# Joint mix of a two-stream transformer kernel: pair-wise attention steps, and 16 modulation units moved to the wide up stage

## The chip, the core and the metric

The kernel runs on one NeuronCore of a Trainium2 chip. TensorE (PE) multiplies matrices into eight PSUM banks of 512 fp32 columns; VectorE (DVE), ScalarE (ACT) and GpSimd (POOL) work on SBUF, the first two on PSUM too; SyncE (SP) issues the DMAs. Each engine runs its own queue in order and waits for the others by semaphores. The metric is the device time of one launch in microseconds (us), as the median of several runs.

## The reference

A transformer on 256 tokens of 1024 features, all in fp32. `first_block` has two layers. `second_block` has two more over two streams, 256 latent and 256 context tokens, each with modulation from a conditioning vector:

```python
mod_l = jnp.split(silu(c) @ ada_w[l] + ada_b[l], 6)          # the same for c_ctx: six parts of 1024
hl = modulate(x_lat, norm_g[l, 0], mod_l[0], mod_l[1])       # rms norm, scale, shift; hc likewise
mix_c, mix_l = even_mixer(hc, hl, ...)                       # layer 0; odd_mixer in layer 1
x_lat = x_lat + mod_l[2] * (mix_l @ w_out[l])
x_lat = x_lat + mod_l[5] * conv_ffn(modulate(x_lat, norm_g[l, 1], mod_l[3], mod_l[4]), ...)
```

`even_mixer` has two halves. One is a bidirectional mLSTM of four heads of width 128, in chunks of 128 tokens: per chunk the query-key products times a decay matrix, the state carried on, and a stabilised division. The other is attention of eight heads of width 64 with a learnt sink in the softmax: the context tokens attend to themselves, the latent tokens to the context and to a window of their own. Its output, the mLSTM's normed output beside it, goes through `w_out`. `conv_ffn` is an up projection to 2 x 2816 features, a depthwise convolution of width 3 on both halves, silu(gate) x value, and a down projection.

## The kernel before, in words

**Products with weights.** All weights stream through a ring of `SLOTS` = 3 slots of 1 MB, issued by SP in the order of the list `issue` (L2902); the DMA into a slot waits until PE has read the slot's former content. Each weight matrix comes in halves. ACT makes the high part of a half (`ahead`, L357; `HIGHS` = 4 halves in flight), GpSimd the low part (`lows_G`, L364), and PE makes three matmuls of each product (`product`, L370 to L372). `done(...)` names the semaphore count of a step that is noted, so that the program's order in each queue is the order in which the Python code writes it.

**Stages.** The layers of the second block are called 2.0 and 2.1. For layer 2.0 the stages are "2.0 in" (projection to the mixers' inputs, six cuts of four pieces for the tiles of 128 tokens, each read out of its bank by DVE, L748, or ACT, L751), "2.0 attention" (the joint mix), "2.0 out", "2.0 ffn up" (22 column blocks f of 2 x 128 features over all 512 tokens) and "2.0 ffn down".

**The joint mix** weaves three generators in each engine's queue (`both_of`): attention, recurrence and modulation, one slot each at a time, 23 slots of recurrence, five per head. In four of five slots there is an attention step too; what is left of attention runs after the recurrence.
- Attention (`att_T`, `att_V`, `att_A`): 32 jobs, one head and one query tile each, first the context stream's 16 (256 keys), then the latent stream's 16 (512 columns, masked). At step s PE makes the scores of job s (L918), the turn (transpose) of job s-3 (L927) and the values' sum of s-4 (L942); DVE takes the minimum of job s (L964, masked L960; signs are turned) and scales the probabilities of s-2 (L975 to L981); ACT makes exp (L1006), the sink's exp (L1009) and copies the turned rows (L1017). Rows have four buffers (`NB`). From job 21 on, scores take three banks in turn and turns two.
- Recurrence (`mlstm_T`, `mlstm_V`, `mlstm_A`): chunk sums (L2060), query-key products (L2069), ACT's decay rows (L2100, L2103), DVE's product with them (L2150) and the finishing steps (L2117 to L2134). Its output goes on over GpSimd (`mout_G`) and DVE (`mout_sum_V`, at given steps of attention, `MOUT_AT`).
- Modulation (`late_mod_T`, `late_mod_V`): `LATE_MOD` lists ten (layer, part) pairs of four units, 40 units of 1 MB. Each is streamed through the ring and multiplied with silu(c) (L1663, 16 matmuls), two or three half units a slot in the loop, by `LATE_TURNS`. A finished part is added to its bias by DVE (`mod_rows_V`, L1683), and parts 0, 1, 3 and 4 are also laid flat by PE and DVE (`mod_flat_T`, `mod_flat_V`). The sums alternate between banks 0 and 6.

**The wide up stage.** `up_T` makes block f into banks 2(f mod 4) and 2(f mod 4)+1, after the hidden low of block f-4 (L1525). `up_A` makes, for each block in this order: the high of half 2f+4 of the stage (in the slot of block f+2), the mids of both halves (L1514), the high of half 2f+5, silu (L1518) and the hidden high (L1520). `up_V_both` makes four convolution steps (L1561, L1564), then the hidden low of block f-1 (L1525), then the product (L1572):

```python
            for f in range(FC):
                ahead(A, m0 + 2 * f + 1 + HIGHS)
                A.eng.wait_ge(tensor_done, done("T", ph, "up", f))
```

**An earlier stage with units behind its blocks.** "1.0 ffn up" (256 tokens) already multiplies eight modulation units behind column blocks; they are streamed into two slots of their own in `work` by DMAs of L2885. Layer 2.1's mixer already uses steps of pairs of heads (`pair_T` L1206, `pair_V`, `pair_A`, `tile_pairs`): its turns are L1221, its scores L1251, its sums L1276.

## Time and profile before

| | |
|---|---|
| time, median of 3 runs | 1874.07 us (1873.81 to 1883.03) |
| the profiled execution: its time | 1877.97 us |
| its span | 1876.1 us |
| mean granted PE clock | 0.98 of full speed |
| first scores of the mix to "2.0 out" | 863.7 to 1043.0 us |
| busy: PE, ACT, DVE, GpSimd | 94%, 48%, 40%, 51% of the span |

A row of the timeline has the start in us from the span's start, the duration, the engine, the line of the kernel, the operation and its tiles; in brackets the time that the engine had stood idle before, and the step that ended it. A matmul row with xN is N matmuls of the same kind in line.

### The profile page before, as it was taken

How to read it: one execution, taken by the hardware profiler on the slowest of the kernel's cores; microseconds unless marked ns; L12 is line 12 of the kernel's file. 1: busy time of each engine (PE TensorE's matmuls, PEld its weight loads, DVE VectorE, ACT ScalarE, POOL GpSimd, SP SyncE). 2: the span in 40 equal slices, each digit the busy share in tenths (PEclk: the TensorE clock that was granted, in tenths of full speed). 3: DMA queues.
4: the chain of work that ended last, by engine and by line, in shares of the span. 5: the costliest groups of instructions: out<-in, count | busy, mean ns of one | idle time of the engine just before them, and what ended most of it. 6: DMA issues, size and time to landing. Idle time of an engine off the chain costs nothing.

```text
span 1876.1 us, 25748 instructions
## 1 busy us (share of the span) xinstructions
PE 1767.1 (94%) x10058; PEld 1438.4 (77%) x10058; DVE 751.9 (40%) x1655; ACT 905.7 (48%) x1654; POOL 947.6 (51%) x416
## 2 busy tenths in 40 slices
PE   8999999998899999898998999999999898899998
PEld 6668998776688888785555888888888877678886
DVE  4543231244344453743567143343200443346631
ACT  4655454445566743433335354444422454457762
POOL 4645688774278885331015234444343341238886
PEclk9999999999899999999999999999999999999999
DMA  8336765443156653227875133333232430136654
GB/s 271 102 102 215 244 186 176 168 157 113 56 163 186 182 177 105 77 90 247 286 275 180 51 85 90 90 109 94 90 101 79 108 106 24 45 92 192 188 169 146
DMA packets 264843, 263.48 MB, mean 140 GB/s; under 512 B 11332, under 2 KB 202124, under 8 KB 264596
## 3 DMA queue, kind: packets, MB, share of 16 engines
q1 hardware_dynamic: 264435, 261.25, 45.0%
q8 instruction: 80, 1.31, 0.3%
q10 hardware_dynamic: 288, 0.59, 0.1%
q14 instruction: 40, 0.32, 0.1%
HBM read 260.76 MB, written 1.06 MB: 140 GB/s over the span
## 4 chain that ended last, share of the span: by engine, by line
PE 80%; DVE 7%; ACT 5%; DMA 5%; issue 2%; SPq 1%; POOL 0%; ACTq 0%; DVEq 0%
PE bank L370 18%; PE bank L371 18%; PE bank L372 17%; PE bank L1447 8%; PE bank L1448 4%; PE bank L1663 2%; PE bank L1251 2%; DMA weights<-in_ada_w 2%; ACT work L1369 1%; PE bank L1221 1%; ACT weights_high L357 1%; PE bank L2060 1%; PE bank L918 1%; PE bank L942 1%; DVE work L1330 1%
## 5 line engine op out<-in xcount | busy, mean ns | idle before, releaser
L364 POOL TENSOR_TENSOR weights_low<-weights,weights_high 128x1024 fp32r<-128x1024 f32 (+1 forms) x388 | 918.7, 2382 | 767.4 <-ACT weights_high L357 766.9
L357 ACT ACTIVATE weights_high<-weights 128x1024 fp32r<-128x1024 f32 (+1 forms) x388 | 401.6, 1046 | 377.8 <-PE bank L372 122.1
L370 PE MATMUL bank<-weights_high,normed_features_high_low 128*128 128x512 f32 (+4 forms) x752 | 288.9, 384 | 14.6 <-POOL weights_low L364 5.6
L372 PE MATMUL bank<-weights_low,normed_features_high_low 128*128 128x512 f32 (+4 forms) x752 | 273.8, 364 | 0.0
L371 PE MATMUL bank<-weights_high,normed_features_high_low 128*128 128x512 f32 (+4 forms) x752 | 273.7, 364 | 0.0
L1447 PE MATMUL bank<-normed_features_high_low,weights_high 128*128 128x512 f32 x704 | 249.4, 399 | 0.6 <-DVE normed_features_high_low L499 0.4
L370 PE MATMUL bank<-normed_features_high_low,weights_high 128*128 128x256 f32 (+1 forms) x704 | 237.9, 338 | 0.4 <-DVE normed_features_high_low L497 0.2
L371 PE MATMUL bank<-normed_features_high_low,weights_low 128*128 128x256 f32 (+1 forms) x704 | 236.5, 336 | 0.0
L372 PE MATMUL bank<-normed_features_high_low,weights_high 128*128 128x256 f32 (+1 forms) x704 | 236.5, 336 | 0.0
L1448 PE MATMUL bank<-normed_features_high_low,weights_low 128*128 128x256 f32 x704 | 197.7, 281 | 0.0
L370 PEld LDWEIGHTS bank<-weights_high,normed_features_high_low 128*128 128x128 f32 x752 | 144.9, 193 | 46.4 <-issue 13.6
L370 PE MATMUL bank<-weights_high,hidden_high 128*128 128x512 f32 x440 | 172.9, 393 | 2.8 <-DVE hidden_low_narrow L1525 1.0
L372 PE MATMUL bank<-weights_low,hidden_high 128*128 128x512 f32 x440 | 171.3, 389 | 0.0
L372 PEld LDWEIGHTS bank<-weights_low,normed_features_high_low 128*128 128x128 f32 x752 | 144.4, 192 | 21.3
L1447 PEld LDWEIGHTS bank<-normed_features_high_low,weights_high 128*128 128x128 f32 x704 | 132.3, 188 | 34.3 <-DVE normed_features_high_low L499 0.5
L371 PEld LDWEIGHTS bank<-weights_high,normed_features_high_low 128*128 128x128 f32 x752 | 145.1, 193 | 17.0
L370 PEld LDWEIGHTS bank<-normed_features_high_low,weights_high 128*128 128x128 f32 x704 | 133.6, 190 | 17.7 <-issue 3.3
L372 PEld LDWEIGHTS bank<-normed_features_high_low,weights_high 128*128 128x128 f32 x704 | 133.6, 190 | 13.6
L371 PEld LDWEIGHTS bank<-normed_features_high_low,weights_low 128*128 128x128 f32 x704 | 133.6, 190 | 13.5
L1448 PEld LDWEIGHTS bank<-normed_features_high_low,weights_low 128*128 128x128 f32 x704 | 133.0, 189 | 0.0
L371 PE MATMUL bank<-weights_high,hidden_low_narrow 128*128 128x512 f32 x264 | 102.8, 389 | 0.0
L370 PEld LDWEIGHTS bank<-weights_high,hidden_high 128*128 128x128 f32 x440 | 82.6, 188 | 23.3 <-POOL weights_low L364 2.2
(330 smaller groups left out, 2334.1 us busy)
## 6 DMA issues: line engine op xcount, KB each, us to landing
weights<-in_ffn_w_up SPq DMA_DIRECT2D x44, 1024.0 KB, 6.1
weights<-in_ffn_up SPq DMA_DIRECT2D x44, 1024.0 KB, 6.0
weights<-in_ada_w SPq DMA_DIRECT2D x40, 1024.0 KB, 6.3
weights<-in_ffn_w_down SPq DMA_DIRECT2D x20, 1024.0 KB, 5.1
weights<-in_ffn_down SPq DMA_DIRECT2D x20, 1024.0 KB, 5.0
weights<-in_diff_w_qkv SPq DMA_DIRECT2D x12, 1024.0 KB, 5.2
weights<-in_hyb_w_in SPq DMA_DIRECT2D x11, 1024.0 KB, 5.5
weights<-in_odd_w_in SPq DMA_DIRECT2D x9, 1024.0 KB, 5.2
```

Source lines behind the costliest of these rows:

```text
L357: A.eng.activation(high(whigh[:, m % HIGHS, :]), raw(wslot[:, u % SLOTS, :]), ACT.Copy).then_inc(scalar_done, A.one(("A", "high", m)))
L364: G.eng.tensor_tensor(raw(wlow[:, u % SLOTS, :]), raw(wslot[:, u % SLOTS, :]), high(whigh[:, m % HIGHS, :]).bitcast(F32), ALU.subtract).th ...
L370: T.eng.matmul(out_, lh, rh, start=first, stop=False)
L371: T.eng.matmul(out_, ll, rh, start=False, stop=False)
L372: return T.eng.matmul(out_, lh, rl, start=False, stop=last)
L918: i = T.eng.matmul(bank[:, a:b], l, r, start=(m == 0), stop=(m == len(terms) - 1))
L942: i = T.eng.matmul(o, l, r, start=(first and c == 0), stop=(last and c == nc_ - 1))
L1221: i = T.eng.transpose(psum[TURNED][:, at:at + P], way["probs"](buffer(way, q, x), n)[:, c * P:(c + 1) * P], ident)
L1251: i = T.eng.matmul(psum[SCORES[x]][:, a:b], l, r, start=(m == 0), stop=(m == len(terms) - 1))
L1447: T.eng.matmul(bank[:, 0:2 * n].rearrange("p (h t) -> p h t", h=2), wh, nTb[:, :, k, lo:lo + n], start=first, stop=False)
L1448: return T.eng.matmul(bank[:, 0:n], wl, nTh[:, k, lo:lo + n], start=False, stop=last)
L1663: i = T.eng.matmul(to[32 * j:32 * j + 32, :], silu_k[:, k, 2 - 2 * layer:34 - 2 * layer], w[:, a, j * MOD_N:(j + 1) * MOD_N], start=(k == ...
```

## The change

1. **Attention of the joint mix by pairs.** The 32 jobs become 16 steps, each of the two heads of one tile (`tile_pairs`). A step has two half-steps, each taking one slot of `both_of`. In the first PE makes the scores of pair s into banks 3 and 4. In the second it turns pair s-1 into bank 0, for 256 columns both heads at once and one wait, for 512 head by head, each after ACT has copied the one before. When s-2 was a group's second tile, it then sums the group over both tiles, 256 columns wide, into bank 7. DVE takes the maxima of s in the first half and scales the probabilities of s-1 in the second; ACT makes exp in the first and copies the turned rows of s-1 in the second. There are two buffers for each head's rows.
2. **Modulation.** `LATE_MOD` has 24 units, one in each of the first 24 calls, all in bank 6, so that a part waits until DVE has read the one before; the flats of four parts come together at the end in bank 5. The other 16, parts 2 to 5 of layer 2.1 (`UP_MOD`), stream through the ring between the weights of blocks 0 to 15 of "2.0 ffn up", one behind each block, and are multiplied behind it into banks 6 and 7. That stage has three blocks in flight in place of four. DVE adds a part's rows at f = 4, 8, 12 and 16.
3. **"2.0 in".** The pieces of cuts 2 and 3 are all read by ACT. ACT makes a weight high between the two directions of the gates' logarithms; the turns L852 of the second group start a slot later; the exp table is loaded ahead of the last copies; the mix's first modulation matmul waits for DVE's last piece only. The DMAs that bring decay rows in come at the first and the third unit.
4. The down stage's and gates' banks of 2.0 are permuted, since banks 6 and 7 are free earliest.

The core of the diff:

```diff
-        LATE_MOD = [(0, i) for i in range(2, 6)] + [(1, i) for i in (0, 1, 3, 2, 4, 5)]
+        LATE_MOD = [(0, i) for i in range(2, 6)] + [(1, i) for i in (0, 1)]
+        UP_MOD = [(1, i) for i in range(2, 6)]
...
+                if f < len(between) * MOD_UNITS:
+                    layer, idx = between[f // MOD_UNITS]
+                    up_unit[f] = len(stream)
+                    stream.append((mod_source(layer, idx, f % MOD_UNITS), mod_view))
+                    issue.append(("weights", len(stream) - 1))
...
-        add_up("2.0 ffn up", io["ffn_up_2"][0])
+        add_up("2.0 ffn up", io["ffn_up_2"][0], between=UP_MOD)
...
+        def att_T(T, ph, steps):
+            count, held = len(steps), None
+            for s in range(count + 3):
+                if s < count:
+                    j = steps[s]
+                    if s >= 1:
+                        e = "V" if steps[s - 1]["mask"] is not None else "A"
+                        T.eng.wait_ge(SEM[e], done(e, ph, "read", s - 1, 1))
+                    for (a, b, terms), (_, _, others) in zip(j["heads"][0]["scores"], j["heads"][1]["scores"]):
...
                 yield
+                if 0 <= s - 1 < count:
+                    q = s - 1
+                    n = steps[q]["n"]
+                    for heads in heads_of(n):
+                        if held is not None:
+                            T.eng.wait_ge(scalar_done, done(*held))
+                        for x in heads:
+                            T.eng.wait_ge(vector_done, done("V", ph, "probs", q, x))
+                            for c in range(n // P):
+                                at = (x * n if len(heads) == 2 else 0) + c * P
+                                i = T.eng.transpose(psum[TURNED][:, at:at + P], rows_of(q, x, n)[:, c * P:(c + 1) * P], ident)
...
+                        held = ("A", ph, "turned", q, heads[-1])
+                if 0 <= s - 2 < count and steps[s - 2]["tile"] == 1:
...
+        def in_flight(ph):
+
+            return 3 if ph == "2.0 ffn up" else 4
...
+                if ph == "2.0 ffn up" and f in up_unit:
+                    up_mod_T(T, f)
+                if ph == "2.0 ffn up" and f - 6 in up_flats:
+                    mod_flat_T(T, *up_flats[f - 6], up_sums(f - 6)[1])
...
+        def up_mod_T(T, f):
+
+
+            (layer, idx), unit, u = UP_MOD[f // MOD_UNITS], f % MOD_UNITS, up_unit[f]
+            T.eng.wait_ge(slot_full[u % SLOTS], 16 * (u // SLOTS + 1))
+            if unit == 0 and f >= 2 * MOD_UNITS:
+                before = UP_MOD[f // MOD_UNITS - 2]
+                T.eng.wait_ge(vector_done, done("V", "mod flat" if before[1] in FLAT else "mod rows", *before))
+            for a in range(2):
+                i = mod_unit_T(T, layer, unit, mod_view(wslot[:, u % SLOTS, :]), a, up_sums(f)[0])
+            i.then_inc(tensor_done, T.one(("T", "slot", u)))
...
+        LATE_TURNS = [2] * 24
...
             for d in range(2):
                 log_sigmoid(None, A, ph, d, None, mrow(d, 2), mrow(d, 3))
+                if d == 0:
+                    ahead(A, first_half["2.0 in"] + 14)
...
-        proj_phase("2.0 in", ("2.0 norm", ALL, shift_scale(0, 0)), EVEN_CUTS, lambda c: ALL, even_dst, lambda c, j: "A" if c == 4 else "VA"[j % 2],
+        proj_phase("2.0 in", ("2.0 norm", ALL, shift_scale(0, 0)), EVEN_CUTS, lambda c: ALL, even_dst, lambda c, j: "A" if c in (2, 3, 4) else "VA"[j % 2],
...
-            both_of(att_V(V, ATTN, js + jl, aside), mlstm_V(V, ML), late_mod_V(V))
+            both_of(att_V(V, ATTN, js + jl, aside), mlstm_V(V, ML), late_mod_V(V), True)
```

## Rows read from the trace of the kernel before

**Rows 1.** The page's head and busy times of the engines.

```profile
span 1876.1 us, 25748 instructions
...
PE 1767.1 (94%) x10058; PEld 1438.4 (77%) x10058; DVE 751.9 (40%) x1655; ACT 905.7 (48%) x1654; POOL 947.6 (51%) x416
```

**Rows 2.** Sums by stretch: us, busy by engine, granted clock, DMA share, GB/s.

```profile
864.00:979.00 115.00, 99.83 (x852) 57.62 (x854) 59.96 (x203) 44.44 (x146) 7.52 (x6) 0.96 0.82 292
979.00:1043.00 64.00, 56.12 (x393) 35.12 (x385) 43.91 (x93) 29.50 (x66) 28.12 (x20) 0.92 0.48 158
1110.00:1360.00 250.00, 250.00 (x1104) 206.96 (x1103) 94.46 (x132) 108.31 (x141) 107.81 (x45) 1.00 0.34 97
919.00:942.50 23.50, 21.81 (x197) 12.86 (x197) 15.42 (x49) 9.24 (x32) 2.50 (x2) 1.00 0.84 298
```

**Rows 3.** Timeline of PE: a gap in "2.0 in", and the first modulation matmul.

```profile
786.67 0.80 PE L370 MATMUL bank<-weights_high,normed_features_high_low 128*128 128x512 f32 x1 [5.43 <-DVE big L748]
...
866.74 0.65 PE L1663 MATMUL bank<-weights,silu_wide 128*32 128x256 f32 x4 [2.36 <-ACT big L751]
```

**Rows 4.** Timeline of PE: first scores, a late job's scores, first product of "2.0 out".

```profile
863.69 0.70 PE L918 MATMUL bank<-qk_features 64*128 64x256 f32 x2
...
979.80 1.12 PE L918 MATMUL bank<-qk_features 64*128 64x512 f32 x2
...
1042.97 0.58 PE L370 MATMUL bank<-weights_high,normed_features_high_low 128*128 128x512 f32 x1
```

**Rows 5.** Timeline of PE in the loop: a modulation unit and chunk sums.

```profile
944.90 1.07 PE L1663 MATMUL bank<-weights,silu_wide 128*32 128x256 f32 x16
...
947.48 2.50 PE L2060 MATMUL bank<-big,work 128*128 128x129 f32 x20
```

**Rows 6.** Timeline of PE in the mix of layer 2.1: turns and sums of pairs.

```profile
1558.57 0.60 PE L1221 MATMUL bank<-con,work 128*128 128x128 f32 x4
...
1567.49 1.95 PE L1276 MATMUL bank<-work,big 128*64 128x256 f32 x16
```

**Rows 7.** Timeline of DVE and ACT in the loop: softmax steps and a decay product.

```profile
906.34 0.42 DVE L964 TENSOR_REDUCE mxs<-bank 128x1 f32<-128x256 f32 x1
...
906.87 0.15 DVE L975 TENSOR_TENSOR mxs<-mxs 128x1 f32<-128x1 f32 x1
...
906.98 0.48 ACT L1006 ACTIVATE attention_rows<-bank,mxs 128x256 f32<-128x256 f32 x1 [3.12 <-DVE mxs L967]
...
909.71 0.69 DVE L2150 TENSOR_TENSOR work<-bank,gate_rows 128x512 f32<-128x512 f32 x1 [0.36 <-ACT gate_rows L2103]
```

**Rows 8.** Timeline of DVE and GpSimd in the mix's tail.

```profile
1020.22 2.23 DVE L975 TENSOR_TENSOR mxs<-mxs 128x1 f32<-128x1 f32 x1
...
1020.08 2.35 POOL L364 TENSOR_TENSOR weights_low<-weights,weights_high 128x1024 fp32r<-128x1024 f32 x1 [1.46 <-ACT weights_high L357]
```

**Rows 9.** DMA issues at 1163.89, 171.00 and 205.6: KB, us to landing.

```profile
weights<-in_ffn_up SPq DMA_DIRECT2D x1, 1024.0 KB, 6.0
...
work<-in_ada_w SPq DMA_DIRECT2D x1, 1024.0 KB, 7.6
...
work<-in_ada_w SPq DMA_DIRECT2D x1, 1024.0 KB, 9.6
```

**Rows 10.** Timeline of SP in "1.0 ffn up": weights and a unit issued in line.

```profile
169.97 0.61 SPq L2902 DMA_DIRECT2D weights<-in_ffn_w_up  x1
171.00 1.51 SPq L2885 DMA_DIRECT2D work<-in_ada_w  x1
```

**Rows 11.** Timeline of ACT and DVE in "2.0 ffn up": one block, and the next block's mids.

```profile
1163.90 0.78 ACT L1514 ACTIVATE gate_rows<-bank,convcol 128x512 f32<-128x512 f32 x1 [3.76 <-PE bank L372]
...
1165.24 1.06 ACT L357 ACTIVATE weights_high<-weights 128x1024 fp32r<-128x1024 f32 x1
...
1167.80 0.68 DVE L1525 TENSOR_TENSOR hidden_low_wide<-bank,hidden_high 128x512 fp32r<-128x512 f32 x1
...
1174.78 1.45 ACT L1514 ACTIVATE gate_rows<-bank,convcol 128x512 f32<-128x512 f32 x2 [3.82 <-PE bank L372]
```

More of the change, by code:

```diff
@@ new lines, in att_V @@
+        def att_V(V, ph, steps, aside):
+            count = len(steps)
+            for s in range(count + 3):
+                if s < count:
+                    j = steps[s]
+                    V.eng.wait_ge(tensor_done, done("T", ph, "turn", s - 2, 1))
+                    for x, head in enumerate(j["heads"]):
+                        b = 2 * (s % 2) + x
+                        mn = mxs[:, b:b + 1]
+                        bank = psum[SCORED[x]][:, 0:j["n"]]
+                        V.eng.wait_ge(tensor_done, done("T", ph, "scores", s, x))
+                        if j["mask"] is not None:
+                            V.eng.tensor_tensor_reduce(out=rows_of(s, x, j["n"]), in0=bank, in1=j["mask"], scale=1.0, scalar=head["sink"],
+                                                       op0=ALU.add, op1=ALU.min, accum_out=mn).then_inc(vector_done, V.one(("V", ph, "read", s, x)))
+                        else:
+                            V.eng.tensor_reduce(mn, bank, AX_X, ALU.min).then_inc(vector_done, V.one())
+                            V.eng.wait_ge(vector_done, V.n)
+                            V.eng.tensor_tensor(mn, mn, head["sink"], ALU.min).then_inc(vector_done, V.one())
+                        V.note(("V", ph, "max", s, x))
@@ L985, in att_V @@
-                if s >= LOW and jobs[s - LOW]["close"] is not None:
-                    j = jobs[s - LOW]
-                    src_cols, high, low = j["close"]
-                    if low is not None:
-                        V.eng.wait_ge(scalar_done, done("A", ph, "group", j["group"]))
-                        V.eng.tensor_tensor(low, psum[SUM_BANK][:, src_cols], high.bitcast(F32), ALU.subtract).then_inc(vector_done, V.one(("V", ph, "group", j["group"])))
-                yield
-        def att_A(A, ph, jobs, aside={}):
-            n = len(jobs)
-            for s in range(n + LOW):
+                yield
@@ new lines, in att_V, with att_A @@
+                if 0 <= s - 3 < count and steps[s - 3]["close"] is not None:
+                    j = steps[s - 3]
+                    cols, high, low = j["close"]
+                    V.eng.wait_ge(scalar_done, done("A", ph, "group", j["group"]))
+                    V.eng.tensor_tensor(low, psum[SUMMED][:, cols], high.bitcast(F32), ALU.subtract).then_inc(vector_done, V.one(("V", ph, "group", j["group"])))
+                yield
+        def att_A(A, ph, steps, aside):
+            count = len(steps)
+            for s in range(count + 3):
+                if s < count:
+                    j = steps[s]
+                    if j["mask"] is None:
+                        A.eng.wait_ge(tensor_done, done("T", ph, "turn", s - 2, 1))
+                    for x, head in enumerate(j["heads"]):
+                        b = 2 * (s % 2) + x
+                        mn = mxs[:, b:b + 1]
+                        A.eng.wait_ge(vector_done, done("V", ph, "max", s, x))
+                        pb = rows_of(s, x, j["n"])
+                        A.eng.activation(pb, pb if j["mask"] is not None else psum[SCORED[x]][:, 0:j["n"]], ACT.Exp, bias=mn, scale=-1.0,
+                                         accum_out=mxs[:, 8 + b:9 + b]).then_inc(scalar_done, A.one(("A", ph, "read", s, x)))
+                        A.eng.activation(mxs[:, 16 + b:17 + b], head["sink"], ACT.Exp, bias=mn, scale=-1.0).then_inc(scalar_done, A.one(("A", ph, "exp", s, x)))
+                if 0 <= s - 3 < count and steps[s - 3]["close"] is not None:
+                    j = steps[s - 3]
+                    cols, dst, _ = j["close"]
+                    A.eng.wait_ge(tensor_done, done("T", ph, "sum", j["group"]))
+                    A.eng.activation(dst, psum[SUMMED][:, cols], ACT.Copy).then_inc(scalar_done, A.one(("A", ph, "group", j["group"])))
@@ L1279, in pair_T @@
                             l, r = (pt, head["v"][c]) if tok else (head["v"][c], pt)
-                            i = T.eng.matmul(psum[SUMMED][rows_, cols], l, r, start=(first and c == 0), stop=(last and c == n // P - 1))
+                            i = T.eng.matmul(psum[way["sum_bank"]][rows_, cols], l, r, start=(first and c == 0), stop=(last and c == n // P - 1))
                     i.then_inc(tensor_done, T.one(("T", ph, "out", q)))
@@ L1792, in gates_A @@
                     A.eng.wait_ge(scalar_done, A.n)
-                    A.eng.activation(gate[:, s * D + half * 512:s * D + half * 512 + 512], psum[bank + 2 * streams.index(s) + half][:, :], ACT.Copy).then_inc(scalar_done, A.one(("A", ph, "gates")))
+                    A.eng.activation(gate[:, s * D + half * 512:s * D + half * 512 + 512], psum[banks[2 * streams.index(s) + half]][:, :], ACT.Copy).then_inc(scalar_done, A.one(("A", ph, "gates")))
         S1 = 3080
```

321 lines of the change are left out of this document (133 added, 188 removed).

## The prediction, made before the changed kernel was run

> **What bounds the kernel now.** I read the page first, then sums by stretch, then the rows of each stage that the change touches. The profiled execution spans 1876.1 us and TensorE (PE) is busy for 94% of it [rows 1]; its reported time is 1877.97, so 1.9 us lie around the span, and the median of the runs is 1874.07, 3.9 below that execution. PE is nearly everywhere the bound, so an edit counts only if it takes work off PE or closes one of PE's gaps. Three stretches matter [rows 2]. In the joint mix the loop over the recurrence's heads (864 to 979) has PE at 99.8 of 115.0 us, with the DMA engines at 0.82 and 292 GB/s (the 40 modulation units); its tail (979 to 1043) has PE at 56.1 of 64.0. In the wide up stage PE is at 250.0 of 250.0 us, while ACT, DVE, GpSimd and the DMA engines are each below half. So the change moves work from a stage where PE has 23 us of gaps to one where PE has none: work moved there costs its full length. That alone is neutral; what decides is what becomes of the gaps.
>
> **"2.0 in".** Before block 786.67 PE stood 5.43 us for DVE's copy of a result bank (L748), and the mix's first modulation matmul waited 2.36 us for ACT's copy (L751) [rows 3]. The change gives four copies of cuts 2 and 3 to ACT, puts a weight high between the two directions of ACT's gate logarithms, and moves the six turns one slot later. DVE's queue ahead of that copy gets shorter, so the 5.43 should go: I take **-5.4** (bound: 0, if ACT, which gets those copies and also the gate work, is then the late one). The wait of 2.36 now hangs on DVE's last copy alone; its gain is counted in the mix.
>
> **The mix, loop.** It runs from the first scores at 863.69 to the scores at 979.80, 116.1 us; out begins at 1042.97, a tail of 63.2 [rows 4]. One head of the recurrence (five slots) is a block of 23.5 us with PE busy 21.8 of it [rows 2]: two groups of chunk sums at 2.50, the recurrence's query-key products, modulation units (16 matmuls) at 1.07, and four attention jobs [rows 5], whose scores cost 0.70 each [rows 4]. After the change PE's work in a block falls: five units for 6.67 take 1.8 us off, and turns for two heads at once and sums over 256 columns for both tiles together take about another 3.5 (turns of four 0.60, wide sums 16 matmuls in 1.95 [rows 6]). That leaves about 16.5 us. If PE stayed the bound the loop would fall by 5 blocks times 7 us = 35, and the tail by some 8 more: -43 is the lower bound.
>
> I don't take it, because buffers shrink with the work. Before, four row buffers let a job's softmax take two steps and its turn three. After, a pair's scores are one half-step ahead of the turn of the pair before, and the two score banks are the same for each pair. So between scores and turn there is a chain that PE's queue must sit out if it hasn't enough in between: DVE's minimum 0.42 and small ops of 0.15 (a 128x256 head), ACT's exp 0.48 with its sums, then reciprocal and scaling on DVE, twice; and in DVE's and ACT's queues stand the recurrence's own steps, 0.69 for a product with the decay matrix [rows 7] and the finishing products. Walking the five slots with these durations, PE waits 1.7 us for the probabilities behind the finishing products in one slot, 3.6 in the slot where scores, minimum, exp, ACT's decay rows, DVE's product and the scaling stand in one line, and 0.5 and 0.6 in two others: 16.5 + 6.4 = 22.9 us for a block. Five blocks save 3 us; the start, where modulation groups of four slots stood before the first sums and the 2.36 wait, saves 6; four waits of the one bank 6 for its rows and two LAT pairs cost about 3, and the sixteen units' absence from slots outside full blocks gives back about 6. The loop comes to about 104: **-12**. The upper bound is +5, if each wait catches one more DVE or ACT step.
>
> **The mix, tail.** The six pair steps of the latent stream (512 columns) turn head by head because of one turn bank; a step needs scores of about 1.1 [rows 4], minimum and mask twice, exp twice, two turns of 0.60 and two copies in line, 6.2 us, with sums of up to 1.95 each second time [rows 6]. DVE and GpSimd collide here already: a 128x1 addition (L975), which takes 0.15 elsewhere [rows 7], took 2.23 while GpSimd's low ran 2.35 [rows 8]. Six steps, the flats, the mout sums and the out highs give about 63, against 63.2: **0** (bounds -8 and +6). The Trainium skill ("SBUF — State Buffer", section "🔬 SBUF: two separate sides") says a DVE op with two SBUF inputs and a GpSimd op that reads SBUF exclude each other for the whole instruction; the row agrees, and by that rule each of the three GpSimd lows left in the tail can hold DVE's now fewer ops once.
>
> **The up stage.** Here 16 units of modulation get in, one behind each of blocks 0 to 15, through the same ring of three slots, and blocks in flight fall from four to three. A unit costs PE 1.07 [rows 5]: 16 x 1.1 = 17.6, with nothing to hide it. Before, the DMA of block f+3 is issued when block f has been read and lands 6.0 us later [rows 9], with blocks 10.88 us apart (mids at 1163.90 and 1174.78 [rows 11]), so well before its use. After, weights W and units M alternate. Let E be the end of block f's products. M of f+1 is issued at E, and W of f+2 needs the slot of M of f, read at E+1.1. Two such DMAs back to back are in the trace only in the first up stage: issued 1.03 apart (169.97, 171.00), the second landed after 7.6 [rows 9, 10], that is 8.65 after the first issue. So W of f+2 lands at about E+8.65. PE needs it only at E+13. But ACT's order is: high of half 2f+4 (which is in W of f+2) **before** the mids of block f. That high now stands at E+8.65 instead of long before, and takes 1.06 [rows 11]; the mids start at E+9.7 where they started at once. From the mids to the end of the hidden low of the block before are 1163.90 to 1168.5, 4.6 us [rows 11]. The low of f is issued behind the convolutions of f+1, so it ends at E(f+1)+14.3, and with three blocks in flight block f+3 waits for it. Its own start would be E(f+1)+P+1.1, with P the period: P must be at least 13.2 where block and unit need only 10.88+1.1 = 12.0. So 14 blocks run at 13.2, 2.3 above before = 32.5, plus two units ahead of them 2.2, one flat and one wait at f=12 for the flat of two parts earlier, 3: **+38**. Bounds: +19 if W lands before E+7.5 (then neither ACT nor the banks are late and only the units count), +47 if it shares some of the delay of the pairs of that stage whose successors were issued before they had landed (second after 9.6 [rows 9], 2.0 later than the one above; I take 0.7 of it, P 13.9, as the end, since here nothing is issued before both are down).
> The price of the pair has another source: the Trainium skill ("DMA: Bandwidth & Descriptors", section "🔬 Anatomy of one DMA — SWDGE (gpsimd) path") gives 2.0 us and bytes over 436 GB/s, by which both megabytes would be down 6.8 us after E. The rows disagree (6.0 for one alone, 8.65 for two, where the formula has 4.4 and 6.8); by the formula there would be no stall and the up stage would be +19.
>
> **Sum.** -5.4 - 12 + 0 + 38 = +20.6 on the profiled execution's 1876.1 us span; the same on the median: 1874.1 + 20.9 = **1895**. The rest of the kernel is unchanged (other down banks and gate banks: same work, banks free long before).
>
> **Rivals.**
> (A) W lands early enough, no up stall. The up stage costs 19: -5 -12 +19 = +2, **1876**. For it: a modulation unit is read in longer pieces than an up block, and the mix took 292 GB/s [rows 2], 7.2 us for two megabytes. Against: the measured pair, and that landing has to be before E+7.5, below it.
> (B) The up stall as forecast, but the mix is bound by PE and not by the chain: -5 -43 +38 = -10, **1864**. For it: DVE is busy 15.4 and ACT 9.2 us of a block of 23.5 [rows 2], so both have room. Against: the softmax chain is in line with one pair ahead, not work in parallel.
> (C) Both: -5 -35 (the loop alone) +19 = -21, **1853**. It is the case that ends on the other side, and its point of decision is whether the pair of DMAs is down by E+7.5 and the chain of scores to turn stays within the 5 us of PE work of a slot.
> (D) Clock: PE's granted clock was 0.96 in the loop and 0.92 in the tail, 1.00 in the up stage [rows 2]. More waiting in the mix can bring more stretches at 1.2 GHz, more stalls in the up stage the first ones there: at 0.97 for the up stage +8, **1903**.
>
> **How the numbers follow.** The likeliest is the forecast with D as its upper part, 0.52 together (1884 to 1914); A has 0.22, B 0.12, C 0.14. The range goes from 1856 to 1914: it takes in A and B whole and leaves out C's lower part and the upper bounds of everything together. A measurement of this kernel tells about 0.5% (9.4 us) from no change: faster than 1864.7 are C and half of B, 0.22; within it A, half of B and little of the forecast, 0.25; slower 0.53.
>
> **What would show it.** In the up stage a period of about 13.2 us between blocks (12.0 if A), PE idle there before L370 for `hidden_low_wide` L1525, and ACT idle ahead of L357 for the DMA of `in_ffn_up`, the mids (L1514) some 9.7 us after a block's end. In the mix about 167 us from the first scores to "2.0 out" against 179.3, PE idle in it released by `attention_rows`. In "2.0 in" no gap of 5 us before the block at 786. The prediction is wrong if up blocks come every 12.0 us, or if the mix falls under 150 us.

## The result, and the profile after

The changed kernel takes **1928.9 us** (median of 4 runs, 1927.4 to 1929.5) against 1875.5 for the one before on the same chip: a ratio of 1.029, with a 95% interval from 1.026 to 1.032. The sign of the forecast was right. The size was not: 53 us slower where 21 were forecast, outside the range that ended at 1914.

The profiled execution spans 1927.7 us against 1876.1. To see where the 51.6 us lie I cut both spans at the same events: the first scores of the mix, the end of the recurrence's last chunk sums (the end of the loop), the first product of "2.0 out", and the first and last product of "2.0 ffn up". (The forecast ended the loop at the scores behind those sums, 0.9 us later.) These are the sums by stretch, with the granted clock behind the busy times. Before:

```profile
863.69:978.87 115.18, 100.01 (x853) 57.82 (x856) 60.18 (x201) 44.65 (x146) 7.52 (x6) 0.96 0.81 291
978.87:1042.97 64.10, 56.22 (x394) 35.18 (x393) 44.00 (x93) 29.50 (x66) 28.12 (x20) 0.92 0.48 159
1094.69:1337.80 243.11, 243.11 (x1089) 201.94 (x1090) 96.95 (x138) 106.86 (x142) 107.89 (x45) 1.00 0.33 91
```

After:

```profile
855.52:973.27 117.75, 82.19 (x677) 46.58 (x680) 54.43 (x173) 42.91 (x136) 7.48 (x6) 0.88 0.66 224
973.27:1056.38 83.11, 49.35 (x209) 28.52 (x209) 34.62 (x82) 29.81 (x66) 28.03 (x20) 0.63 0.04 13
1108.09:1391.80 283.71, 267.89 (x1353) 210.57 (x1354) 98.91 (x145) 105.11 (x142) 106.94 (x45) 0.99 0.47 137
```

| stretch | before | after | difference | forecast |
|---|---|---|---|---|
| up to the first scores | 863.7 | 855.5 | -8.2 | -5.4 |
| loop of the mix | 115.2 | 117.8 | +2.6 | -12 |
| tail of the mix | 64.1 | 83.1 | +19.0 | 0 |
| "2.0 out" to the up stage's first product | 51.7 | 51.7 | 0 | 0 |
| "2.0 ffn up" | 243.1 | 283.7 | +40.6 | +38 |
| rest | 538.3 | 535.9 | -2.4 | 0 |

The up stage came out as forecast. The mix did not: it lost 22 us where 12 were to be won, and most of that lies in its tail, where PE's granted clock is 0.63 and PE is busy for 49 of 83 us, less than before in spite of the low clock. Of the 31 us between the forecast +20.6 and the measured +51.6, 19.0 lie in the tail and 14.6 in the loop; the up stage adds 2.6, "2.0 in" and the rest take 5.2 off.

**The up stage's rows.** Block 1 shows the whole mechanism (SP, ACT, DVE and PE timelines of the changed kernel):

```profile
1135.02 0.37 SPq L2937 DMA_DIRECT2D weights<-in_ada_w  x1
1136.06 0.61 SPq L2937 DMA_DIRECT2D weights<-in_ffn_up  x1
...
1144.20 1.06 ACT L365 ACTIVATE weights_high<-weights 128x1024 fp32r<-128x1024 f32 x1 [5.53 <-DMA weights<-in_ffn_up]
1145.16 0.76 ACT L1526 ACTIVATE gate_rows<-bank,convcol 128x512 f32<-128x512 f32 x1
...
1149.04 0.68 DVE L1537 TENSOR_TENSOR hidden_low_wide<-bank,hidden_high 128x512 fp32r<-128x512 f32 x1
...
1149.78 0.50 PE L378 MATMUL bank<-normed_features_high_low,weights_high 128*128 128x512 f32 x1 [1.64 <-DVE hidden_low_wide L1537]
```

The unit's DMA goes out as the block ends, the weights' 1.04 us later; these land after 8.1 more. ACT stands 5.53 us for them, makes the high, and only then the mids that [rows 11] show right behind the block; the low follows 4.6 us after the mids, and PE waits for it. By the waits of the two engines in that stage:

```profile
ACT weights_high L365 <- DMA weights<-in_ffn_up: 106.9, 18, 11.9
...
PE bank L378 <- DVE hidden_low_wide L1537: 12.6, 9, 2.2
PE bank L1684 <- DVE modcol L1719: 3.2, 1, 3.2
```

**The mix's rows.** What PE waited for, first in the loop, then in the tail (us in total, times, longest):

```profile
PE bank L939 <- DVE attention_rows L987: 20.6, 9, 4.2
PE bank L1684 <- DMA weights<-in_ada_w: 6.3, 2, 5.3
PE bank L1684 <- DVE mod L1704: 4.9, 2, 4.5
...
PE bank L939 <- DVE attention_rows L987: 24.6, 6, 6.4
PE bank L939 <- ACT big L1027: 4.5, 4, 2.3
PE bank L939 <- ACT attention_turned L1027: 2.2, 3, 0.7
```

Before, the probabilities cost PE no wait in the loop worth a line and 6.1 us in the tail. The other two kinds of wait were there before, with 7.6 and 2.2 us in the loop:

```profile
PE bank L1663 <- DMA weights<-in_ada_w: 7.6, 7, 1.8
...
PE bank L1691 <- DVE mod L1683: 2.2, 1, 2.2
```

In all PE stood 35.6 us in the loop against 15.2, and was busy for 82.2 against 100.0. One step of the tail in full, PE's timeline, and ahead of it the scores of a pair while the clock was still full:

```profile
974.20 1.13 PE L925 MATMUL bank<-qk_features 64*128 64x512 f32 x4
...
1009.35 2.08 PE L925 MATMUL bank<-qk_features 64*128 64x512 f32 x4
1015.14 1.09 PE L939 MATMUL bank<-con,attention_rows 128*128 128x128 f32 x4 [3.72 <-DVE attention_rows L987]
1016.98 1.11 PE L939 MATMUL bank<-con,attention_rows 128*128 128x128 f32 x4 [0.75 <-ACT attention_turned L1027]
1018.02 3.68 PE L950 MATMUL bank<-big 128*64 128x256 f32 x16
```

Everything in it stands in one line, scores, wait, turn, wait, turn, sums, and each of PE's pieces has nearly twice the length that it was priced by: turns 1.09 against 0.60, sums 3.68 against 1.95 [rows 6], scores 2.08 against 1.13. (The price of about 1.1 for a pair's scores came from two matmuls of one head [rows 4]; four of a pair take 1.13 at full clock, so it held.)

DVE's piece of that line is longer too. The scaling of a pair (two instructions) took 1.68 to 2.51 us in four of seven cases in the tail, and 0.88 in the other three; in the four, GpSimd was at the recurrence's output:

```profile
1013.90 2.51 DVE L987 TENSOR_SCALAR attention_rows<-attention_rows,mxs 128x512 f32<-128x512 f32 x2
1026.21 0.88 DVE L987 TENSOR_SCALAR attention_rows<-attention_rows,mxs 128x512 f32<-128x512 f32 x2
...
1014.80 1.33 POOL L2217 TENSOR_TENSOR big<-big,head_g 128x512 f32<-128x512 f32 x1
```

Together the four took 4.9 us more than four times 0.88, in PE's line. The longest wait of the tail, 6.39 us before the turn at 994.58, has DVE's sum of the recurrence's output (0.68) and the flats' copies (2.5 us, from 990.27 to 992.76) between the reads and the scaling. The change had moved these sums to pair steps 11 to 14 (`MOUT_AT`), which the list of the change leaves out. No experiment takes them away.

### The profile page after: what moved, and what is told of

It reads as the page before. It is cut to its first block, busy times and chain, and to the rows that moved or that the text cites. A ratio compares the mean times of both kernels' runs of the same rounds, so it can differ in the third digit from the quotient of the medians.

```text
span 1927.7 us, 25465 instructions
## 1 busy us (share of the span) xinstructions
PE 1763.4 (91%) x9962; PEld 1427.8 (74%) x9962; DVE 737.6 (38%) x1619; ACT 905.1 (47%) x1650; POOL 947.2 (49%) x416
## 4 chain that ended last, share of the span: by engine, by line
PE 71%; DVE 11%; ACT 8%; DMA 6%; issue 3%; POOL 1%; SPq 1%; DVEq 0%; ACTq 0%
PE bank L378 17%; PE bank L379 16%; PE bank L380 16%; PE bank L1451 5%; DMA weights<-in_ffn_up 3%; ACT weights_high L365 2%; PE bank L1452 2%; PE bank L1255 2%; PE bank L1684 2%; ACT work L1373 1%; PE bank L1225 1%; PE bank L2092 1%; PE bank L950 1%; PE bank L939 1%; DVE qk_features L1583 1%
## 5 line engine op out<-in xcount | busy, mean ns | idle before, releaser
L378 PE MATMUL bank<-normed_features_high_low,weights_high 128*128 128x256 f32 (+1 forms) x704 | 241.0, 342 | 13.0 <-DVE hidden_low_wide L1537 12.6
L378 PEld LDWEIGHTS bank<-weights_high,normed_features_high_low 128*128 128x128 f32 x752 | 144.4, 192 | 39.3 <-issue 13.6
L380 PEld LDWEIGHTS bank<-weights_low,normed_features_high_low 128*128 128x128 f32 x752 | 144.3, 192 | 21.4
```

The costliest lines, as they stand in the source:

```text
L378: T.eng.matmul(out_, lh, rh, start=first, stop=False)
L380: return T.eng.matmul(out_, lh, rl, start=False, stop=last)
```

## The experiments

Two theories for the tail stood at the outset. **P**: the granted clock. PE stands idle so much that it is granted 1.2 GHz for most of the stretch, and the priced durations double. **R**, the rival, that the line of semaphores alone sets the step. For the up stage: **W**, the weights land late for ACT, against **B**, three blocks in flight are too few.

Ratios are against the kernel before, which ran beside each group of experiments with medians of 1872.6 to 1874.1 us; the changed kernel did not, so a few us between its 1928.9 and a time below say little. The stages differ less: where their code is the same, the loop took 117.8 to 119.6 us, the tail 83.1 to 83.6, the stalled up stage 280.6 to 288.6.

### The clock: matmuls that compute nothing

```diff
+                    if s >= 12:
+                        warm_T(T, 1, 14)
                     for heads in heads_of(n):
```

> The changed kernel with 14 small matmuls of the identity (128 columns, into bank 1, which nobody reads then) in front of each turn of pair steps from step 12 on, that is in the gaps of 2.5 to 3.7 us in which TensorE waits for the scaled probabilities in the tail of the joint mix. They compute nothing; everything else is as it was. Theory P (price of the clock): the tail costs 83.1 us instead of the forecast 63 because TensorE stands idle so much that its granted clock falls to about 0.5 to 0.67 there and turns take 1.09 for 0.60, scores 2.08 for 1.13, sums 3.7 for 1.95. With the gaps filled the granted clock of the stretch after the mLSTM should rise above 0.85 and the time should FALL by 10 to 17 us although work was added. Theory Q (chain of semaphores): the softmax chain alone sets the step, TensorE's durations don't matter; then the added matmuls change nothing or cost up to 7 x 1 us.

Measured: 1917.4 us, 11.5 less than the changed kernel, for 70 matmuls more (14 in each of five steps; the trace has two records for each). The loop is the same 117.8; the tail:

```profile
971.04:1044.90 73.86, 53.58 (x349) 38.69 (x349) 34.75 (x82) 29.79 (x66) 28.14 (x20) 0.84 0.04 15
```

9.2 us less at a granted clock of 0.84 for 0.63 (I had put it above 0.85; before the change it was 0.92). Theory P holds for about half of the 19 us. The added matmuls begin with the third pair step of the tail, and from there on a step is near its forecast, by PE's timeline:

```profile
1006.15 1.13 PE L926 MATMUL bank<-qk_features 64*128 64x512 f32 x4
...
1014.84 1.13 PE L926 MATMUL bank<-qk_features 64*128 64x512 f32 x4
...
1021.77 1.13 PE L926 MATMUL bank<-qk_features 64*128 64x512 f32 x4
```

That is 8.7 us with sums and 6.9 without, for 12.3 and 8.1 to 8.3 in the changed kernel, and for 8.2 and 6.2 in the forecast. The two steps ahead of it took 27 us from scores to scores in both kernels (971.97 to 998.85 here, 974.20 to 1001.07 there), with waits of 4.7 and 6.4 us for the probabilities; by my reading the ten us that remain stand mostly there. Whether matmuls added there too would take them away wasn't tried.

### The up stage: order of ScalarE, and no second DMA

Highs last, in "2.0 ffn up" alone:

```diff
-                ahead(A, m0 + 2 * f + 1 + HIGHS)
                 A.eng.wait_ge(tensor_done, done("T", ph, "up", f))
...
                 A.eng.activation(hidh(f, n), up_hidden(ph, f, n), ACT.Copy)...
+                ahead(A, m0 + 2 * f + 2 + HIGHS)
```

> The changed kernel with one order changed in 2.0 ffn up alone: ScalarE makes the two weight highs of block f+2 behind the silu and the hidden high of block f, not ahead of its mids. Theory W (weights late for ScalarE): from the end of block 0 to the end of block 21 the stage takes 269.0 us against 228.8 before; 17 to 19 are the units, some 21 are mids that stand behind a high whose weights land 8.65 us after the block. With the order turned the stage should take 247 to 250 us, and the kernel 19 to 22 us less. Theory B (three blocks in flight are too few in themselves): the stage stays over 260.

Measured: 1907.7 us, 21.2 less. The stage fell by 17.8 us, to about 251 on the expectation's scale, just above its 247 to 250:

```profile
1109.62:1375.50 265.88, 264.36 (x1353) 208.27 (x1354) 98.93 (x145) 106.27 (x141) 103.56 (x44) 1.00 0.50 147
```

The stalls are gone, 1.5 us of waits are left, none of them for the hidden low.

The units' matmuls on token rows, nothing streamed:

```diff
-                    stream.append((mod_source(layer, idx, f % MOD_UNITS), mod_view))
-                    issue.append(("weights", len(stream) - 1))
...
-                i = mod_unit_T(T, layer, unit, mod_view(wslot[:, u % SLOTS, :]), a, up_sums(f)[0])
+                i = mod_unit_T(T, layer, unit, mod_view(x_t[:, 0:SLOT]), a, up_sums(f)[0])
```

> The changed kernel, but the 16 modulation units of 2.0 ffn up are not streamed: their matmuls read the token rows in SBUF in place of the weights (so layer 2.1's parts 2 to 5 are computed from the wrong data; the work on TensorE is the same). The ring then carries the stage's own weights only. Theory W: without the second DMA per block the weights of f+2 are long there, the stage takes 228.8 + 16 x 1.1 = 246 to 249 us, 20 less than the changed kernel's 269.0. Theory B (three blocks in flight): stays over 260, since banks and matmuls are the same.

Measured: 1908.6 us, and 264.24 us for the stage with PE busy in all of it:

```profile
1107.26:1371.50 264.24, 264.24 (x1353) 208.23 (x1354) 98.94 (x145) 107.05 (x142) 108.00 (x45) 1.00 0.30 84
```

Both runs say the same by different ways: theory W, not B. Three blocks in flight cost nothing by themselves; what four would have cost with late weights was not run. They also give the price of the units with no stall in it: 264.2 - 243.1 = 21.1 us for 16 units with two flats, 1.3 each, where I had 1.1 and 3 for the rest. (The two expectations quote 269.0 and 228.8 for the distance from the first block's end to the last one's; the stretches in the fences begin a block earlier.)

### "2.0 in" alone

```diff
-... lambda c, j: "A" if c == 4 else "VA"[j % 2],
+... lambda c, j: "A" if c in (2, 3, 4) else "VA"[j % 2],
```
with the high in `mgate_A`, the later turns and the earlier exp table, on the kernel before. The DMAs of the decay rows and the wait of the first modulation matmul are those of before.

> The kernel before with the edits of 2.0 in alone: pieces of cuts 2 and 3 all read by ScalarE, a weight high between the gates' two directions, turns one slot later, exp table ahead of the last copies. The joint mix and the up stage are those of before. In the changed kernel the first scores of the mix came 8.2 us earlier, 5.4 of it the gap at 786 that went and, by my reading, 2 to 3 more of it because the granted clock between 786 and 830 was 0.91 to 0.93 instead of 0.82 to 0.89. Expected: first scores at 855 to 856 instead of 863.7 and the whole time 5 to 9 us below before. Rival: the mix takes it back since its first modulation units find fewer landed DMAs; then under 3 us less.

Measured: 1866.5 us (10 runs), ratio 0.995, interval 0.9935 to 0.9969; first scores at 857.7, a little later than the 855 to 856 expected. This part is a gain of 0.5%, and the mix behind it doesn't take it back (loop 116.0, tail 61.8), though PE now stands 5.07 us for modulation weights at its start:

```profile
866.87 1.94 PE L1663 MATMUL bank<-weights,silu_wide 128*32 128x256 f32 x16 [5.07 <-DMA weights<-in_ada_w]
```

The first scores come at 851.0 to 857.7 in the twelve traces of kernels with these edits, so the gain in front of the mix, 6 to 13 us, is known no better than that.

### The two large parts, each alone

Units alone: before's attention, `UP_MOD` and three blocks in flight.

```diff
-        LATE_TURNS = [4, 2, 2] + [3, 3, 2] * 7 + [2] * 8
+        LATE_TURNS = [4, 2, 2] + [3, 3, 2] * 5
```

> The kernel before with one part of the change alone: the 16 modulation units go to 2.0 ffn up with three blocks in flight; attention stays in 32 single-head jobs, 24 units stay in the mix at the old pace (so they end after 18 slots). Up stage as in the changed kernel: 265 to 270 us for the 21 block periods against 228.8, +40. Theory N (units filled gaps and held the clock): the mix gets shorter by less than the 16 units' 17 us, 0 to 10 us. Theory L (TensorE-bound mix): shorter by 15 to 17 us. So the kernel is 24 to 40 us slower than before; if it comes out near the changed kernel (+53), pairs brought nothing at all, if clearly faster, the pairs cost time.

Measured: 1902.4 us, ratio 1.016 (1.011 to 1.021). Up stage 279.6 (+36.5); loop 108.0 (-7.2), tail 58.1 (-6.0). The 16 units leave the mix with 13 us, a little more than the 0 to 10 of theory N and less than theory L's 15 to 17.

Pairs alone (with "2.0 in"): all 40 units in the mix, four blocks in flight.

```diff
-        LATE_MOD = [(0, i) for i in range(2, 6)] + [(1, i) for i in (0, 1)]
-        UP_MOD = [(1, i) for i in range(2, 6)]
+        LATE_MOD = [(0, i) for i in range(2, 6)] + [(1, i) for i in (0, 1, 3, 2, 4, 5)]
+        UP_MOD = []
...
-        LATE_TURNS = [2] * 24
+        LATE_TURNS = [4, 2, 2] + [3, 3, 2] * 7 + [2] * 8
```

> The changed kernel with the modulation units put back: all 40 in the joint mix (the old pace: 64 half units in the 24 slots of the loop, 16 in the tail), none in 2.0 ffn up, four blocks in flight there and the banks of before for the down stage. Pairs and the edits of 2.0 in stay. Up stage back to 228 to 230 us (-40). The mix: if its time is chain and clock (theory P), the units fill gaps: 195 to 205 us against the changed kernel's 200.9, so the kernel takes 1885 to 1895; if TensorE's work simply adds, 200.9 + 17 = 218, and the kernel takes about 1905.

Measured: 1893.5 us; up stage back at 243.1; the mix 121.3 + 83.2 = 204.5, 3.6 more than in the changed kernel although 16 units are in it again, and within the expectation for theory P, as the whole time is. There they lie mostly in the gaps. The tail, with eight of them, has the same 83 us as without, at a granted clock of 0.75 for 0.63:

```profile
979.05:1062.22 83.17, 54.40 (x345) 31.01 (x345) 36.61 (x87) 29.67 (x66) 28.03 (x20) 0.75 0.34 114
```

Against the kernel with the edits of "2.0 in" alone (mix 116.0 + 61.8) the pairs cost 5.3 us in the loop and 21.4 in the tail. So each part is a loss of its own: the units, 36.5 us in the up stage with 13.2 given back in the mix, and the pairs as written, some 27 us in the mix.

### What the pairs' line hangs on: order on VectorE

In the changed kernel `att_V` reads pair s in the first half-step and scales pair s-1 in the second. The turn of s-1 is therefore behind the scores of s and their reads, and being one pair ahead overlaps nothing. The edit, in short:

```diff
+                if s >= 12:
+                    scale_V(V, ph, steps, s - 1)     # den, reciprocal, two tensor_scalar
                 if s < count:
                     j = steps[s]
                     ...                              # the reads of pair s
                 yield
-                if 0 <= s - 1 < count:
+                if s < 12 and 0 <= s - 1 < count:
                     ...                              # the same scaling
```

> The changed kernel with one order changed on VectorE, from pair step 12 on (the tail): the probabilities of pair s-1 are scaled ahead of the reads of pair s, not behind them. In the changed kernel a step of the tail is one line: scores of s, two masked reads 1.5 us, scaling of s-1 1.2, turn, copy 0.75, turn, sums, scores of s+1, so that being one pair ahead overlaps nothing. Theory R (order on VectorE): with the scaling first, scores of s run beside it, and the tail falls from 83 us by 12 to 20. Theory P alone (clock): the line has its length from TensorE's 1.2 GHz; the reorder takes off only the 1.5 us of reads in each of six steps, 9 us at most, at the same granted clock of 0.63.

Measured: 1920.3 us; tail 76.8, 6.3 less, at a granted clock of 0.67. Less than theory R's 12 and within what theory P allowed. The wait had moved. In the tail of this kernel:

```profile
PE bank L939 <- DVE attention_rows L966: 11.1, 2, 6.4
PE bank L939 <- ACT big L1033: 8.9, 4, 3.3
PE bank L939 <- ACT attention_turned L1033: 7.7, 3, 4.6
```

The first line's two waits are at the start of the tail; they are the steps ahead of the edit. For the rest PE now waits 16.6 us (6.7 in the changed kernel) for ACT's copies out of the one turn bank, which by the program's order stand behind the exps of the next pair in ACT's queue.

With the idle matmuls too (6 in each step, the same diff as the first experiment):

> As the kernel before this one (scaling first from step 12 on), with 6 matmuls of the identity into bank 1 in front of each turn of these steps as well. If clock and order are two causes that add up, the tail falls to 60 to 66 us, the level of the kernel before the change (64.1), with a granted clock over 0.85. If the order alone keeps TensorE busy enough, the added matmuls make no difference, within 3 us.

Measured: 1924.1 us, tail 74.5 at 0.77. The expectation of 60 to 66 failed: by my reading clock and order don't add up as long as the copies hold PE, 12.1 us here. The tail won 2.3 us on the run before, more than the 0.5 by which equal tails differ; the whole time is 3.9 longer all the same, since the profiled execution's up stage, whose code is unchanged, took 288.6 against 280.6.

In all steps (`s >= 1` for `s >= 12`):

> The changed kernel with VectorE's scaling ahead of the reads in all pair steps, in the loop over the recurrence too. In the loop TensorE stands 20.6 us for attention_rows in nine waits. Theory R: these waits fall to under 10 us, the loop from 117.8 to about 107. Rival: in the loop the scaling now waits for ScalarE's exp in front of the recurrence's own steps on VectorE, and the loop stays within 3 us of 117.8 while the tail gains as in the run with the tail alone.

Measured: 1901.5 us, 27.4 less than the changed kernel; **the loop falls from 117.8 to 101.4** with a granted clock of 0.92, the tail to 72.9. PE has no wait for the probabilities left in the loop. The rival came true in part: the waits for the recurrence's own product on DVE, 2.3 us in the changed kernel, are 11.2 here:

```profile
PE bank L2107 <- DVE work L2188: 9.2, 4, 2.9
...
PE bank L2098 <- DVE work L2188: 2.0, 1, 2.0
```

The same with all 40 units in the mix:

> Pairs with scaling first in all steps, all 40 modulation units in the mix and none in 2.0 ffn up (four blocks in flight), edits of 2.0 in kept. Against the same kernel with the scaling behind (median 1893.5): if order is what pairs lacked, the mix falls from 204.5 to about 180, and the kernel to 1868 to 1875, level with the kernel with the edits of 2.0 in alone (1866.5). If pairs cost something else (the single turn bank, the single modulation bank), it stays above 1880.

Measured: 1872.9 us (10 runs), ratio 0.999, interval 0.997 to 1.001: loop 113.0, tail 73.0, together 186 where 180 were expected. Level with the kernel before, as expected, but 6 above "2.0 in" alone: the loop is 3.0 shorter than there, the tail 11.2 longer.

### The second turn bank, and both placements of the units

```diff
-        SCORED, TURNED, SUMMED = (3, 4), 0, 7
+        SCORED, SUMMED = (3, 4), 7
+        TURNED = lambda q, x: 1 if q >= 11 and x == 1 else 0
```

> The kernel with pairs, scaling first, all 40 units in the mix (median 1872.9, tail 73.0 us) and one thing more: from pair step 11 on the second head is turned into bank 1, so that its turn doesn't wait for ScalarE's copy of the first. In that tail TensorE stands 17.7 us for these copies, in seven waits. Theory S (single turn bank): half of it or more goes, the tail is 62 to 67 us, and the kernel takes 1862 to 1868, below the one before the change. Rival: ScalarE's copies stand behind the exps of the next pair anyway, in its queue; then the wait moves to the next step's turn and the tail stays above 70.

Measured: **1856.7 us** (6 runs), ratio **0.991**, interval 0.989 to 0.993: below both kernels, and 9.7 below "2.0 in" alone. The tail is 59.9 us at a granted clock of 0.86, better than the 62 to 67 expected. In the step shown, turns of both heads run in one piece, at full clock, with units before them:

```profile
996.48 1.13 PE L926 MATMUL bank<-qk_features 64*128 64x512 f32 x4
997.54 1.07 PE L1692 MATMUL bank<-weights,silu_wide 128*32 128x256 f32 x16
998.54 1.09 PE L941 MATMUL bank<-con,attention_rows 128*128 128x128 f32 x8
999.56 1.95 PE L952 MATMUL bank<-big 128*64 128x256 f32 x16
1001.44 1.07 PE L1692 MATMUL bank<-weights,silu_wide 128*32 128x256 f32 x16
1002.44 1.13 PE L926 MATMUL bank<-qk_features 64*128 64x512 f32 x4
```

Six us from scores to scores, with two units in them; eight turns take what four took at 1.2 GHz.

The changed kernel with all three orders mended and the units still in the up stage:

> The changed kernel, 16 units still in 2.0 ffn up, with the three orders repaired: ScalarE's highs last in that stage, scaling first in all pair steps, second turn bank in the tail. If the causes add up: 1929 - 21 (highs) - 27 (scaling) - 3 to 8 (bank) = 1873 to 1878, still not below the one before, as 16 units at 1.3 us in a stage without gaps cost 21 us there. If it comes below the sibling with the units in the mix, moving the units was right and only the orders were wrong.

Measured: 1874.5 us (12 runs), ratio 1.000 (0.999 to 1.002), as the sum of the causes had it. Side by side with the former:

| | loop | tail | up stage | median |
|---|---|---|---|---|
| units in the mix | 113.2 | 59.9 | 243.2 | 1856.7 |
| units in the up stage | 100.9 | 60.2 | 266.0 | 1874.5 |

The units cost 12.3 us in the loop, nothing in the tail, and 22.8 in the up stage. So moving them was a loss of its own even with these orders right. (The medians are 17.8 us apart and these differences make only 10.8: the trace of the former is its longest execution of six, that of the latter its shortest of twelve.) The tail of the second shows something more: 60.2 us, 22.9 less than in the changed kernel, at a granted clock of only 0.77:

```profile
952.90:1013.11 60.21, 39.73 (x209) 24.59 (x209) 35.39 (x82) 28.40 (x66) 27.96 (x20) 0.77 0.06 19
```

The two edits of the line, without any matmul added for the clock, take off more than the whole 19 us.

## Why the prediction was wrong

**Right.** "What bounds the kernel": moving work from a stage with gaps into one without costs its full length. The up stage was forecast at +38 and came at +40.6 by the named mechanism: weights landing 8.65 us after the block's end by forecast, 9.2 measured (1135.02 to 1144.20); mids behind the high; the low 4.6 us later; PE waiting for it with three blocks in flight. Periods between the mids of blocks 1 to 14 lay between 11.6 and 16.1 us, 13.6 on average, around the forecast 13.2. Rivals A and C, early weights, fell, and with them the prediction's estimate of 6.8 us for the two by the Trainium skill's formula ("DMA: Bandwidth & Descriptors", section "🔬 Anatomy of one DMA — SWDGE (gpsimd) path"). That formula is a fit for DMAs issued by GpSimd; these are issued by SP. The terms inside were off and cancelled in part: PE's work grew by 24.8 us (21.1 where nothing stalls) for the 18 or so priced, it waited 12.6 us for the lows for about 17, and 3.2 for the flat of two parts earlier for about 2. "2.0 in": -8.2 for -5.4; the gap went, and the clock behind it rose, from 0.83 between 780 and 820 us to 0.94 and 0.89 in its two halves, which the sum had left out.

**The tail, forecast 0, measured +19.** This is the failed step. The line of a step was seen, "in line, 6.2 us, with sums of up to 1.95 each second time", but all PE's pieces in it were priced by rows at full clock. In the steps of the tail PE stood 4.5 us of 8.7, or of 12.3 with sums; the granted clock fell to 0.63 on the whole, and the low clock lengthened the line in turn: from turn to turn steps took 7.5 to 14.6 us. The clock was among the rivals, yet for the up stage only, at 8 us, where it stayed at 0.99. The added matmuls give 9.2 us as the clock's part with the line as it is, and with them a step takes 6.9 and 8.7 us. The line itself is set by two choices, the reads ahead of the scaling and the single turn bank. With both mended the tail is 60 us, below the 64 of the kernel before, though the clock is 0.77 to 0.86. The forecast of 63 for the tail as written was thus what a mended order gives, not what a serial step at 1.2 GHz gives. The prediction had expected DVE and GpSimd to collide over three lows; they collided over the recurrence's output, 4.9 us in the scalings alone.

**The loop, forecast -12, measured +2.6.** The waits in a block were walked right: 1.7 + 3.6 + 0.5 + 0.6 by forecast, and 3.60, 1.73 and 1.59 from 888.72 to 913.67. The sum around them failed. It took 3 us off for five blocks of 23.5 us, which are already the whole loop (117.5 of 116.1), and then 6 more for "slots outside full blocks". Five blocks at the forecast 22.9 us are 114.5 and not 104. The trace has 33.2 us to the second chunk sums of the first head, for 37.6 before (the start, forecast -6), and then three heads in 81.4 us for 75.1: 25.0, 29.6 and 26.9 each. Of the 29.6, 4.5 us are the wait for the single modulation bank (all such waits together 4.9, 2.2 before, where part of 3 was allowed). The clock, 0.88 for 0.96, is again in no term. Modulation weights that had not landed cost 6.3 us, but 7.6 before, so they are no part of the difference. "The sixteen units' absence gives back about 6" was near with attention as it was: the loop gave back 7.2 us (units alone); with the orders mended it is 12.

**The sums.** The line of the sum gives +20.6, and the next adds 20.9; 14 periods of 2.3 are 32.2 and not 32.5; "faster" is C and half of B, 0.20 and not 0.22. None of it matters here.

**What follows for rival B.** It said that the mix could be bound by PE with the chain harmless. As the kernel was written that was wrong, but the order alone takes 16.4 us off the loop. Most of the chain lay in the order of one queue, not in the data.

**Open.** How the 19 us of the tail divide between clock and line isn't settled: 9.2 went with the clock raised alone, 6.3 with the order in the tail alone, 8.6 with both, and 22.9 with the order everywhere and the second bank, at a clock that rose only to 0.77. The waits of the first two steps, 4.7 and 6.4 us, and the collisions with GpSimd were not tested by themselves. Why modulation weights come late at the start of the mix is open too. The decay rows' DMAs stand between other units' in SP's queue since the change, but the kernel with the edits of "2.0 in" alone keeps their old place and has a wait of 5.07 us there, so they can't be the only reason.

## What to carry to other kernels

Work goes to where the bound engine has gaps: the same 16 units cost 12 us in a mix with gaps and 23 in a stage without. Before a chain is priced, ask at which clock it will run: here steps in which the matrix engine stood 4.5 us of 8.7 ran at 1.2 GHz, and rows at full clock gave little more than half of each of its pieces. And where a pipeline is to be "one ahead", check each engine's queue for it: an engine that reads item s before it finishes item s-1 has undone it. Here that one order was worth 27 us, as much as the regrouping had cost.

## What was not expected of the hardware

70 matmuls that compute nothing made the kernel 11.5 us faster, by raising the granted clock of a stretch of 74 to 83 us from 0.63 to 0.84. The Trainium skill ("TensorE: Matmul & The Clock Gate", section "HAM oscillation — how this bites in real kernels") tells of a kernel in which each burst of matmuls is shorter than the wait for its data and starts at the low clock again. The tail here agrees: behind waits of 3.72 us its turns take 1.09 us. And with 40 modulation units in the mix instead of 24, eight of them in the tail, that tail took 83.2 us for 83.1, at a clock of 0.75: there the work in the gaps was free. Neither was it expected that a scaling of two heads' rows on VectorE takes 0.88 us alone and up to 2.51 beside GpSimd's work.
